# Inverse of the unit lower triangle: 16-wide diagonal blocks by substitution on VectorE, the rest by levels on TensorE

## The reference, cut to what matters

```
a_mat = lower + I                      # lower: strictly lower triangular, (k beta) k^T * decay
rhs   = [v_beta, k_beta * exp(g)]
sol   = triangular_solve(a_mat, rhs, lower=True, unit_diagonal=True)
u, w  = sol
for each chunk c:                      # in order: the scan
    v_new = u_c - w_c @ state
    o_c   = (q_c exp(g_c)) @ state + qk_intra_c @ v_new
    state = state * exp(g_last) + k_dec^T @ v_new
```

## Time and profile before

| what | value |
|---|---|
| median of 3 runs | 1255.23 us (1254.22 to 1256.02) |
| profiled execution, its own time | 1253.36 us |
| its span | 1251.9 us |
| its mean granted TensorE clock | 0.962 |
| TensorE matmul / weight load busy | 1157.2 us (92%) / 933.2 us (75%) |
| VectorE, ScalarE, GpSimd busy | 659.6 (53%), 446.0 (36%), 131.4 us (10%) |
| span of stages 0 to 3 of the second block | from about 764 to 1186 us |

### The profile page before, as it was taken

How to read it: one execution, slowest core, us unless ns; L and a number is a source line. 1 busy time by engine, 2 the same in 40 slices (tenths; PEclk the granted TensorE clock), 3 DMA queues, 4 the chain that set the end, 5 groups by cost and what they waited for, 6 DMA issues and landing times.

```text
span 1251.9 us, 14198 instructions
## 1 busy us (share of the span) xinstructions
PE 1157.2 (92%) x5632; PEld 933.2 (75%) x5632; DVE 659.6 (53%) x1071; ACT 446.0 (36%) x742; POOL 131.4 (10%) x106
## 2 busy tenths in 40 slices
PE   6999999999989999999999988888789879878898
PEld 5777878788768888888888865677578668767776
DVE  5545353546256887777522246425654652555474
ACT  5232222344343444444422233322523342342331
POOL 1000000000210000000000000132032122203310
PEclk9999999999989999999999978899899988988999
DMA  8121212112321333323223321110111111111101
GB/s 324 53 69 65 82 55 83 58 61 84 111 75 66 104 109 111 102 88 98 84 101 101 101 97 51 51 34 34 34 51 34 34 51 35 34 34 36 37 31 68
DMA packets 25313, 91.63 MB, mean 73 GB/s; under 512 B 2848, under 2 KB 3104, under 8 KB 25120
## 3 DMA queue, kind: packets, MB, share of 16 engines
q1 hardware_dynamic: 23040, 83.90, 20.3%
q0 software_dynamic: 768, 4.53, 0.9%
q10 hardware_dynamic: 1440, 2.31, 0.5%
HBM read 88.63 MB, written 2.10 MB: 72 GB/s over the span
## 4 chain that ended last, share of the span: by engine, by line
PE 78%; DVE 11%; ACT 6%; issue 4%; POOL 1%; DMA 0%; ACTq 0%; DVEq 0%
PE PS L485 18%; PE PS L488 18%; PE PS L486 18%; PE PS L712 3%; PE PS L578 2%; PE PS L770 2%; ACT Wh L1548 1%; PE PS L600 1%; DVE Wl L948 1%; PE PS L767 1%; DVE C L1436 1%; PE PS L919 1%; PE PS L921 1%; PE PS L920 1%; PE PS L513 1%
## 5 line engine op out<-in xcount | busy, mean ns | idle before, releaser
L485 PE MATMUL PS<-Hh,Wh 128*128 128x512 f32 x856 | 359.1, 419 | 2.1 <-DVE Hl L1130 2.1
L488 PE MATMUL PS<-Hh,Wl 128*128 128x512 f32 x856 | 340.6, 398 | 0.0
L486 PE MATMUL PS<-Hl,Wh 128*128 128x512 f32 x856 | 339.4, 397 | 0.0
L948 DVE TENSOR_TENSOR Wl<-raw,Wh 128x1024 fp32r<-128x1024 f32 x156 | 190.0, 1223 | 206.2 <-ACT Wh L1548 205.0
L485 PEld LDWEIGHTS PS<-Hh,Wh 128*128 128x128 f32 x856 | 164.8, 193 | 47.8 <-issue 16.1
L488 PEld LDWEIGHTS PS<-Hh,Wl 128*128 128x128 f32 x856 | 164.0, 192 | 36.6
L1548 ACT ACTIVATE Wh<-raw 128x1024 fp32r<-128x1024 f32 x156 | 162.3, 1049 | 67.1 <-PE PS L488 48.1
L486 PEld LDWEIGHTS PS<-Hl,Wh 128*128 128x128 f32 x856 | 165.0, 193 | 28.5 <-issue 0.7
L485 PE MATMUL PS<-Ah,Wh 128*128 128x512 f32 x176 | 69.8, 396 | 0.0
L486 PE MATMUL PS<-Al,Wh 128*128 128x512 f32 x176 | 69.8, 396 | 0.0
L488 PE MATMUL PS<-Ah,Wl 128*128 128x512 f32 x176 | 69.8, 396 | 0.0
(11 more groups left out here) (290 smaller groups left out, 1752.2 us busy)
## 6 DMA issues: line engine op xcount, KB each, us to landing
raw<-in_w_units SPq DMA_DIRECT2D x156, 512.0 KB, 3.4
X<-in_x SPq DMA_DIRECT2D x4, 512.0 KB, 6.5
relb<-in_rel POOLq DMA_DIRECT2D x1, 2048.0 KB, 10.2
out<-X ACTq DMA_DIRECT2D x8, 256.0 KB, 2.0
mats<-in_mats POOLq DMA_DIRECT2D x1, 832.0 KB, 4.8
window<-in_window POOLq DMA_DIRECT2D x1, 544.0 KB, 13.0
rope<-in_rope POOLq DMA_DIRECT2D x1, 512.0 KB, 5.2
wgrp<-in_wgrp POOLq DMA_DIRECT2D x1, 256.0 KB, 10.9
```

The costliest lines, as they stand in the source:

```text
L485: pe.matmul(bank, Wh[:, s, w], rhs[0](r), start=first and j == 0, stop=False)
L486: pe.matmul(bank, Wh[:, s, w], rhs[1](r), start=False, stop=False)
L488: ins = pe.matmul(bank, Wl[:, s, w], rhs[0](r), start=False, stop=last and end)
L948: dv.tensor_tensor(Wl[:, s, :], raw[:, s, :], Wh[:, s, :].bitcast(F32), sub).then_inc(unit_split, 1)
```

## The change: what it does

Three edits.

First, levels 1 to 3 (and the level 0 of before) go. Instead, after LT is there, VectorE masks it to the 16 x 16 diagonal blocks with minus signs, sums over the block index so that each column's own block is left (Lc, 128 x 4 x 16), adds the place of the diagonal, and ScalarE's queue stores Lc to DRAM (32 KB). When that has landed, ScalarE's queue loads it back as Lb, each block of 16 partitions getting all 16 rows of its block (128 x 1024, 512 KB, over the storage of TiT and Y). VectorE then makes row after row of the blocks' inverse, two dependent instructions a row (one product, one reduction), 15 rows; spreads them to TiT; TensorE turns TiT, ScalarE copies it to Ti, and levels 4 to 6 go on as before. GpSimd's masks are now three a head.

Second, the paces: PACE_PREP 0.95 to 1.3, PACE_FIRST 1.1 to 1.2. In stages 1 to 3 TensorE's steps are now: K K^T 26, TiT turned 32, level 4 in 34, 5 in 38, 6 in 42, K turned and q k 46, u and w 48. In stage 0: K K^T 11, TiT turned 17, level 4 in 19, u and w 33.

Third, scan and diff come before pair norms and prep in each round, on all engines.

```diff
-PACE_SCALARS, PACE_SCORES, PACE_PREP, PACE_END, PACE_FIRST = 3, 1.7, 0.95, 1.5, 1.1
+PACE_SCALARS, PACE_SCORES, PACE_PREP, PACE_END, PACE_FIRST = 3, 1.7, 1.3, 1.5, 1.2
...
-            yield
-            yield
-            pe.wait_ge(*prep_dv.at(i, "lt"))
-            turn_tiles(b6, LT).then_inc(*prep_pe.tick(i, "turned"))
+            yield from idle(6)
+            pe.wait_ge(*prep_dv.at(i, "tt"))
+            turn_tiles(b6, TiT).then_inc(*prep_pe.tick(i, "turned"))
...
-            return own + ([scan(st, b), diff(st, b)] if b is not None else [])
+            return ([scan(st, b), diff(st, b)] if b is not None else []) + own
...
# VectorE, behind lt
+            dv.tensor_tensor(tiles(Y[:]), tiles(LT[:]), over_tiles(mat(K_MINUS_T)),
+                             mult).then_inc(*prep_dv.tick(i, "masked"))
+            dv.wait_ge(*prep_dv.at(i, "masked"))
+            dv.tensor_reduce(Lc[:], Y[:].rearrange("p (t b i) -> p t i b", b=NB, i=BL), AXX,
+                             add).then_inc(*prep_dv.tick(i, "packed"))
+            dv.wait_ge(*prep_dv.at(i, "packed"))
+            dv.tensor_tensor(Lc[:], Lc[:], own_place, add).then_inc(*prep_dv.tick(i, "lc"))
+            dv.tensor_copy(Tc[:], own_place).then_inc(*prep_dv.tick(i, "tc"))
+            yield
+            yield
+            yield
+            dv.wait_ge(blocks_loaded, 16 * (i + 1))
+            dv.wait_ge(*prep_dv.at(i, "tc"))
+            for r in range(1, BL):
+                if r > 1:
+                    dv.wait_ge(*prep_dv.at(i, ("row", r - 1)))
+                dv.tensor_tensor(Tm[:, :, 0:r + 1],
+                                 Lb[:, 0:r + 1, :, r:r + 1].rearrange("p k t one -> p t (k one)"),
+                                 Tc[:, :, 0:r + 1], mult).then_inc(*prep_dv.tick(i, ("terms", r)))
+                dv.wait_ge(*prep_dv.at(i, ("terms", r)))
+                dv.tensor_reduce(Tc[:, :, r:r + 1], Tm[:, :, 0:r + 1], AXX,
+                                 add).then_inc(*prep_dv.tick(i, ("row", r)))
+                if r % 5 == 0 and r + 1 < BL:
+                    yield
+            dv.wait_ge(*prep_dv.at(i, ("row", BL - 1)))
+            dv.tensor_tensor(
+                TiT[:].rearrange("p (t b i) -> p t b i", b=NB, i=BL),
+                Tc[:].unsqueeze(2).to_broadcast([P, NT, NB, BL]),
+                mat(K_BLOCKS).rearrange("p (b i) -> p b i", i=BL).unsqueeze(1).to_broadcast(
+                    [P, NT, NB, BL]), mult).then_inc(*prep_dv.tick(i, "tt"))
...
# ScalarE, behind the squares
+            yield from idle(7)
+            ac.wait_ge(*prep_dv.at(i, "lc"))
+            ac.dma_start(lower_blocks[i], Lc[:].rearrange("p t i -> p (t i)")).then_inc(blocks_stored, 16)
+            yield
+            yield
+            ac.wait_ge(blocks_stored, 16 * (i + 1))
+            if i:
+                ac.wait_ge(*prep_dv.at(i - 1, ("terms", BL - 1)))
+            ac.dma_start(
+                Lb[:].rearrange("p k t i -> p (k t i)"),
+                lower_blocks[i].rearrange("(b k) n -> b (k n)", k=BL).unsqueeze(1).to_broadcast(
+                    [NB, BL, BL * NT * BL])).then_inc(blocks_loaded, 16)
+            yield
+            yield
+            yield
+            yield
             ac.wait_ge(*prep_pe.at(i, "turned"))
-            ac.activation(Lo[:], b6, ACT.Copy).then_inc(*prep_ac.tick(i, "lo"))
-            yield
+            ac.activation(Ti[:], b6, ACT.Copy).then_inc(*prep_ac.tick(i, "ti"))
```

More of the change, by code:

```diff
@@ L64 @@
 N_COLS = C_GNORM + 4
-(K_ID, K_UPPER, K_HALVES, K_SWAP, K_NEG_T, K_STRICT_T, K_LEVEL) = range(7)
-N_LEVELS = 7
-N_MATS = K_LEVEL + 1 + N_LEVELS
+(K_ID, K_UPPER, K_HALVES, K_SWAP, K_NEG_T, K_STRICT_T, K_BLOCKS, K_MINUS_T, K_PLACE, K_LEVEL) = range(10)
+BL, NB = 16, P // 16
+FIRST_LEVEL, N_LEVELS = 4, 7
+N_MATS = K_LEVEL + N_LEVELS - FIRST_LEVEL
 R_ALOG, R_DT, R_LAM = 0, GH, 2 * GH
@@ L237, in program @@
         sb("head_" + n, [P, S]) for n in ("Vb", "DT", "LT", "Lo", "LmT", "Ti", "TiT", "Y"))
+    place[0] -= 2 * 2048
+    Lb = sb("Lb", [P, BL, NT, BL])
     QG, UU, Wt, Kd, AT, VN, Oa = (
@@ L241, in program @@
         sb("head_" + n, [P, S]) for n in ("Qb", "Kr", "Vd", "Vdt", "Od", "Wd"))
-    Bm = Lm = Y
+    Bm = Y
     Kb = Lo
@@ L351, in program @@
     qk_ac = steps("qk_scalar", ["Kr", "Qb"])
-    levels = range(1, N_LEVELS)
+    levels = range(FIRST_LEVEL, N_LEVELS)
     prep_pe = steps("prep_tensor", ["g", "b", "sums", "vt", "kr", "kk", "turned", *(
         x for lv in levels for x in (("y", lv), ("t", lv))), "kt", "qk", "u", "w"])
-    prep_dv = steps("prep_vector", ["gs", "d", "bm", "dt", "ms", "vb", "kn", "lt0", "lt", "tt", "ti",
+    prep_dv = steps("prep_vector", ["gs", "d", "bm", "dt", "ms", "vb", "kn", "lt0", "lt", "masked", "packed",
+                                    "lc", "tc", *((x, r) for r in range(1, BL)
+                                                  for x in ("terms", "row")), "tt",
                                     *(("t", lv) for lv in levels), "kd", "at", "rq", "wt"])
-    prep_ac = steps("prep_scalar", ["eg", "dt", "silu", "sq", "lo", *(("y", lv) for lv in levels),
+    prep_ac = steps("prep_scalar", ["eg", "dt", "silu", "sq", "ti", *(("y", lv) for lv in levels),
                                     "u"])
-    prep_gp = steps("prep_gpsimd", ["rk", "rq", ("lm", 0), "l0", *(("lm", lv) for lv in levels),
+    prep_gp = steps("prep_gpsimd", ["rk", "rq", *(("lm", lv) for lv in levels),
                                     "qg"])
+    blocks_stored, blocks_loaded = semaphore("blocks_stored"), semaphore("blocks_loaded")
     pair_pe, pair_dv = steps("pair_norm_tensor", ["sums"]), steps("pair_norm_vector", ["ms", "q"])
@@ L2134, in _layout @@
     mats = [i == j, i <= j, i // HD == j // HD, (i // 64 == j // 64) & ((i % 64 + 32) % 64 == j % 64),
-            np.where(i <= j, 0.0, NEG), i < j]
-    for lv in range(N_LEVELS):
+            np.where(i <= j, 0.0, NEG), i < j, i // BL == j // BL,
+            np.where((i // BL == j // BL) & (i < j), -1.0, 0.0), i % BL == j % BL]
+    for lv in range(FIRST_LEVEL, N_LEVELS):
         b = 1 << lv
-        low = (i // (2 * b) == j // (2 * b)) & (i // b > j // b)
-        mats += [low, low.T] if lv == 0 else [low.T]
+        mats.append((j // (2 * b) == i // (2 * b)) & (j // b > i // b))
     mats = np.stack([m.astype(np.float32) for m in mats], axis=1)
```

34 lines of the change are left out of this document (13 added, 21 removed).

## The result

The changed kernel takes 1277.05 us (median of 4 runs, 1275.57 to 1277.51) against 1255.38 before (4 runs): ratio 1.0188, 95% interval 1.0143 to 1.0233. Slower, as forecast, but by 21.7 us where the forecast had 7.6, and outside its range. The profiled execution took 1277.51 us, its span is 1276.1, so 24.2 more than the span before. Some executions fall into a slower state and are left out of the ratios, so a ratio can differ by some thousandths from the quotient of two medians.

The account below looks back on a forecast made before the run. It took TensorE as the bound, 78% of the span. Stages 1, 2, 3, 0 at +2.1, +1.2, +2.1, +4.5 and order -0.9 gave +9.0 on 1253.4, 1262.4; forecast median 1263 us, range 1251 to 1271.

Parts of the forecast that it names:

- The load, "so I take 3.4": 512 KB load of Lb, priced like weight loads of the same size at 3.4 us, bounds 2.0 and 6.5.
- The rival that named the cause: Load from 8 blocks moved by 8 of 16 DMA engines: 1.4 us more a stage, 1269 us; chance 0.27.
- Mask, packing, Lc: +4.6: VectorE's mask and packing reduction after LT: Lc ready 4.6 us after K K^T starts, bounds +4.2 and +5.3.
- The store, +6.7: 32 KB store of Lc to DRAM: 2.0 us plus 0.2 for issues, ending 6.7 us after K K^T starts.
- Rows and spreading, 8.6 us from first row to TiT: VectorE's 30 dependent row instructions, 7.05 us, with output norm's reading 0.75 and spreading to TiT 0.73, in stages 1 to 3.
- The rival of cheap rows: VectorE's dependent row instructions follow in 0.14 us, rows take 4.2 us, kernel 1251 to 1252 us; chance 0.20.
- From TiT to level 4, 2.0: Turning TiT 0.5 us and two products 1.4, hiding ScalarE's copy to Ti: level 4 at +20.8 in stages 1 to 3.
- another term, 6.7 us in all: Low TensorE clock behind the idle stretch before TiT's turning: 2.0 us a stage, 0.7 in stage 2.
- Work from the first level on, and the clock: Less TensorE work from first level on: 10.8 us a stage, 12.4 in stage 0; clock adds 2.0, or 0.7 in stage 2.
- the rival that it goes away there: Low clock behind the pair norms in stages 0 and 2 goes away: 6.8 us less, about 1256 us; chance 0.13.
- The order, -0.9: Scan and diff first in a round: VectorE's state clearing 0.3 us earlier in three stages, 0.9 us gained.
- The pace: Faster pace gives cover to small waits on ScalarE's copy and Kd, about 1.6 us a stage.

Follow-up runs that it names:

- e2: Changed kernel with each head's load reading weights in another source form: 128 rows, 8 x 16 rows, 16 rows each 8 times, 8 rows each 16 times; 1268.88 us, time not used.
- e3: Changed kernel with all four loads plain, 128 different rows from weights, so numbers are others; 1259.96 us, ratio 1.0064.
- e9: Changed kernel with Lc stored twice, so the load reads 16 source rows, each for 8 partitions; 1271.41 us, ratio 1.0162.
- e12: Changed kernel with 22, 13, 14, 13 unread filler products in stages 0 to 3 in TensorE's wait for TiT; 1275.46 us, ratio 1.0189.
- e1: Kernel before with only scan and diff put first in each round; 1245.15 us, ratio 0.9959.
- e7: Changed kernel with the old order in a round, pair norms and prep first; 1282.56 us, ratio 1.0226.
- e11: Kernel before with scan and diff first and the change's paces 1.3 and 1.2, without the new inverse; 1261.67 us, ratio 1.0064.
- e13: Changed kernel with the old paces, 0.95 and 1.1; 1278.88 us, ratio 1.0217.
- e5: Changed kernel with rows spread by VectorE masks and TensorE products into PSUM in place of the transfer through DRAM; 1254.52 us, ratio 1.0023.
- e6: Changed kernel with neither store nor load, rows reading the rope tables, so numbers are others; 1250.17 us, ratio 0.9960.
- e10: e5 with TiT's turning, its copy and the levels three rounds later; 1253.44 us, ratio 0.9995.
- e16: e10 with the paces 1.1 and 1.1 in place of 1.3 and 1.2; 1234.87 us, ratio 0.9869.

## Why the prediction was wrong

The direction was right, and so was the shape: one wait at the turning of TiT, behind VectorE's spreading. The step that failed is the size of the load. By the prediction's own terms, on the profiled executions:

- **The load, "so I take 3.4".** It took 6.6, 7.8, 7.9 and 8.2 us, 16.9 more than four times 3.4. This is the step that failed. The rival that named the cause (a source of 8 blocks is moved by 8 engines) had the mechanism right; e2, e3 and e9 show it. It had only the price wrong: I worked out +1.4 us from eight more packets an engine at the mean packet time of 0.176, where e2 shows 7.7 against 3.5 and 4.7; in head 0 the packets alone spread over 1.9 us more, and each takes longer. Hence the range ended too low as well: my bound of 6.5 for the load was below all four, and four loads at that bound, 12.4 us more, would have given 1275, which my range of up to 1271 did not even hold. The Trainium skill, page "DMA: Bandwidth & Descriptors", section "Why a DMA increments its semaphore by 16 and not by 1", has the rule that the outermost dimensions on both sides decide the number of engines, and the packet counts of e3 agree with its eight.
- **Mask, packing, Lc: +4.6.** Measured +4.6. The reduction took 1.06 us for my 0.69. GpSimd's mask took 1.80 us beside it, and VectorE's took 0.69 all the same.
- **The store, +6.7.** The load's issue comes at +6.1, 1.45 us behind the store's: 0.6 less.
- **Rows and spreading, 8.6 us from first row to TiT.** Measured 8.3 in stages 1 to 3. The rival of cheap rows was wrong: 15 pairs took 7.1 us without the reading between, for my 7.05. In stage 0 it took 11.8 us, where I had 9.7.
- **From TiT to level 4, 2.0.** Measured 3.5 in all stages, 6.1 us more: turning and products ran at the low clock, and where it was held up (e12, stage 2) it took 1.8. I had charged the clock in another term, 6.7 us in all, but that term was needed again behind level 4 (below), so this is a second miss, of the clock.
- Together, the first level comes 15.9, 16.3, 16.3 and 20.4 us later (stages 1, 2, 3, 0) where I had 10.9, 11.3, 10.9 and 14.9: 20.9 us more than forecast: 16.9 of the load, 6.1 of the low clock before level 4, 2.1 of stage 0's rows, less 4.2 for the store, the other rows and the product in stage 0. (In my list 6.7 + 3.4 is 10.1 and not 10.2; it changes nothing.)
- **Work from the first level on, and the clock.** Level 4 to the end of w takes 27.1, 29.8, 29.2 and 30.0 us in stages 0 to 3; my terms (the old stretch, less 12.4 or 10.8, and the clock) give 29.4, 28.4, 31.2 and 28.7. Right within 1.6 us in the sum, but two stages were forecast 2.0 to 2.3 us too long and two 1.3 to 1.4 too short, so that is partly luck. The low clock does not stand behind the wait alone, as I wrote. In the changed kernel it also falls for 3.4 to 6.9 us behind the pair norms, in all four stages, and in e12, which held it up in the wait, it fell there too. So the rival that it goes away there was wrong as well. Its reading of before was also off: stage 0 has 3.4 us at the lower level behind the pair norms and 3.4 more 14 us later, stage 2 has 6.8.
- **The order, -0.9.** As a wait it was right. Over the three stretches from the end of w to the next K K^T, TensorE is idle 28.2 us before, 27.2 in e1 and 27.4 in the changed kernel. But its busy time there, on the same instructions, is 154.2, 149.1 and 148.5 us: the granted clock is 0.94, 0.92 and 0.89 before, and 0.94 to 0.97 in the changed kernel. So the rest of the span got 5.0 us shorter where I had 0.9, by the clock, and that hid part of the load's miss. In e7 the same stretches have 29.9 us idle and 152.1 busy. The clearing of the state is not the reason: TensorE waits 4.5 us for it at L829 in e7, and in the changed kernel 1.0 us for it and 3.0 at the same line for VectorE's step on gs.
- **The pace.** I gave it 1.6 us a stage of gain by cover. On the kernel before it costs 1% (e11), in the changed kernel nothing that was measured (e13).
- **"The wait of VectorE for the load costs nothing by itself"** holds while the load is slow. e5 and e6 show its price once it is fast: other steps of VectorE and one wait for GpSimd then stand before the rows, 2 to 3.4 us.
- **All together:** 9.0 forecast, and 16.9, 6.1, 2.1, -4.2, -1.6 and -4.1 of misses, make the 24.2 us of the spans. All but the load cancel to -1.7. That e3, with a plain load, came out at my forecast is therefore in part luck.

What stays open: why the low clock comes behind the pair norms in some stages and not in others of the same kernel (e10: 49.7 and 46.4 us); the kernel before does the same from run to run, 1246 us at a mean clock of 0.967 and 1262 at 0.955. Why the order of the chains moves it is open too. And e16 was timed in 4 runs, so its interval is wide.

## What to carry to other kernels

Price a DMA by the shape of its source, not by its bytes: 512 KB in 8 outer entries took twice the time of 512 KB in 128, and on a serial path that is the kernel's time. Where a small tile must reach other partitions in the middle of a chain, VectorE's masks and products with a 0/1 matrix did it in 2.8 us without leaving the core. When a chain gets shorter or moves, the products that fill its gaps must be dealt out anew; the inverse by substitution was a loss of 1.9% on one schedule and transfer, and a gain of 1.3% on another, each with the 0.4% in it that the order alone gives. When a gain comes without a shorter wait, look at busy time and clock before naming a cause.

## What the runs showed of the hardware

- A load of 512 KB took 3.5 us from issue to the waiting instruction with 128 source rows, 4.7 with 16 rows given 8 times each, and 7.7 with an outermost dimension of 8, repeated or not (e2; a weight load ran beside it, and without one the changed kernel's took 6.6). The issue's own record grows too: 0.33, 0.62, and 0.64 to 1.20 us.
- Of such a load's 4 KB packets at most 11 were under way at once with 8 source rows (median 0.26 us each), 19 with 128 (0.16 us), both in head 0, changed kernel and e2.
- The store of 32 KB let the next issue go 1.45 us behind its own.
- A dependent pair of VectorE steps on 8 to 64 elements took 0.40 us at the start and 0.54 at the end, about as much from PSUM as from SBUF (0.41 and 0.40 us for the second pair in the changed kernel and in e5).
- Fillers that raised TensorE's clock through a wait (0.93 for 0.71, busy 20.6 of 23.4 us) did not keep it for all that follows: from the turning to the end of w 0.89 with fillers, 0.88 without.
